# Prompt attention over three strided branches of 75 key blocks a head in place of one masked pass of 136

## The reference

```python
DILATIONS = ((128, 1), (512, 4), (2048, 16))
    parts = [dilated_branch_prompt(qb, kb, vb, w // d, d) for w, d in DILATIONS]
...
def merge_dilations(parts):
    ms = jnp.stack([m for _, m, _ in parts])
    mx = jnp.max(ms, axis=0)
    wts = jnp.exp(ms - mx)
    num = sum(wts[i][..., None] * parts[i][0] for i in range(len(parts)))
    den = sum(wts[i] * parts[i][2] for i in range(len(parts)))
    return num / den[..., None]
```

## Time and profile before

| | before |
|---|---|
| median of 3 runs | 2519.24 us |
| span of the profiled execution | 2518.4 us |
| TensorE busy | 2218.1 us, 88% |
| VectorE busy | 933.1 us, 37% |
| ScalarE busy | 770.4 us, 31% |
| GpSimd busy | 315.0 us, 13% |
| stage `mixers` | 1102.5 to 2071 us |

### The profile page before, as it was taken

How to read it: one execution, slowest core, us unless ns; L and a number is a source line. 1 busy time by engine, 2 the same in 40 slices (tenths; PEclk the granted TensorE clock), 3 DMA queues, 4 the chain that set the end, 5 groups by cost and what they waited for, 6 DMA issues and landing times. The chain is left out here.

```text
span 2518.4 us, 40099 instructions
## 1 busy us (share of the span) xinstructions
PE 2218.1 (88%) x13254; PEld 1826.2 (73%) x13254; DVE 933.1 (37%) x2542; ACT 770.4 (31%) x1793; POOL 315.0 (13%) x332
## 2 busy tenths in 40 slices
PE   4787989899989989449998999899989986799997
PEld 3676878687868768139897989798979884466664
DVE  5440133114212411235454545455554544132221
ACT  5321122112112211124444444353534442222221
POOL 5200000000000000111111111111212114111110
PEclk9988999999999999769998999999999995899999
DMA  4526352735456373570404040404040104464641
GB/s 134 160 79 200 108 184 72 218 104 169 142 153 180 79 211 98 65 160 27 101 27 102 26 102 27 102 27 101 26 102 26 35 22 133 138 192 133 192 142 59
DMA packets 197558, 274.10 MB, mean 109 GB/s; under 512 B 37237, under 2 KB 159605, under 8 KB 188677
## 3 DMA queue, kind: packets, MB, share of 16 engines
q1 hardware_dynamic: 188852, 204.74, 30.9%
q0 software_dynamic: 1280, 66.98, 7.8%
q10 hardware_dynamic: 7248, 0.03, 0.2%
HBM read 201.70 MB, written 136.87 MB: 134 GB/s over the span
## 5 line engine op out<-in xcount | busy, mean ns | idle before, releaser
L265 PE MATMUL pj<-hT_hi,w_hi 128*128 128x512 f32 (+1 forms) x1056 | 427.9, 405 | 20.4 <-DVE w_lo L470 20.4
L266 PE MATMUL pj<-hT_lo,w_hi 128*128 128x512 f32 (+1 forms) x1056 | 417.0, 395 | 0.0
L267 PE MATMUL pj<-hT_hi,w_lo 128*128 128x512 f32 (+1 forms) x1056 | 416.0, 394 | 0.0
L1173 ACT ACTIVATE pt<-pt_ps 128x512 f32<-128x512 f32 (+2 forms) x320 | 170.9, 534 | 425.4 <-PE pt_ps L1116 425.2
L1124 PEld LDWEIGHTS o_ps<-vt,pt 128*128 128x128 f32 x2176 | 284.5, 194 | 18.6 <-issue 7.4
L1124 PE MATMUL o_ps<-vt,pt 128*128 128x64 f32 x2176 | 284.0, 271 | 0.0
L1251 DVE CUSTOM_DVE_ANT_0 sc<-s_ps,win 128x512 f32<-128x512 f32 (+2 forms) x320 | 193.0, 610 | 175.0 <-PE s_ps L1100 138.0
L265 PEld LDWEIGHTS pj<-hT_hi,w_hi 128*128 128x128 f32 (+1 forms) x1056 | 198.5, 188 | 67.7 <-DVE w_lo L470 18.2
L267 PEld LDWEIGHTS pj<-hT_hi,w_lo 128*128 128x128 f32 (+1 forms) x1056 | 198.1, 188 | 47.4 <-issue 0.6
L266 PEld LDWEIGHTS pj<-hT_lo,w_hi 128*128 128x128 f32 (+1 forms) x1056 | 198.7, 188 | 42.3 <-issue 0.6
L1167 ACT ACTIVATE sc<-sc,nmax 128x512 f32<-128x512 f32 (+2 forms) x320 | 207.9, 650 | 36.2 <-DVE nmax L1255 36.2
(11 more groups left out here) (358 smaller groups left out, 3190.5 us busy)
## 6 DMA issues: line engine op xcount, KB each, us to landing
out_dram<-in_cache_k_win_dram POOLq DMA_DIRECT2D x8, 4088.0 KB, 15.3
out_dram<-in_cache_v_win_dram POOLq DMA_DIRECT2D x8, 4088.0 KB, 27.7
w_raw<-in_w_in_dram SPq DMA_DIRECT2D x35, 512.0 KB, 9.6
qk_ch<-sil SPq DMA_DIRECT2D x32, 256.0 KB, 6.9
z_ch<-xr SPq DMA_DIRECT2D x32, 256.0 KB, 2.5
wqk<-hi SPq DMA_DIRECT2D x32, 256.0 KB, 3.2
wqk<-lo SPq DMA_DIRECT2D x32, 256.0 KB, 3.5
out_dram<-xr SPq DMA_DIRECT2D x32, 256.0 KB, 2.8
```

The lines of the kernel that those rows point to most:

```text
L265: pe.matmul(out, w_hi[s][:, k, 0:m], hT_hi[:, k, cols], start=(k == 0), stop=False)
L266: pe.matmul(out, w_hi[s][:, k, 0:m], hT_lo[:, k, cols], start=False, stop=False)
L267: mm = pe.matmul(out, w_lo[s][:, k, 0:m], hT_hi[:, k, cols], start=False, stop=(k == KT - 1))
L1173: act.activation(pt[:, n % 4, 0:w], pt_ps[turned_bank((step, qb, *a[1:]))[0]][:, 0:w], ACT.Copy).then_inc(S["turned_out"], 1)
```

## The change

Each branch becomes a banded attention of its own. A query tile is 128 tokens at stride 1, 4 or 16 (`tile_tokens`); it reads its own key tile and, in branches 0 and 1, the one before, so 31 + 28 + 16 = 75 key blocks. Strided tiles are read straight from `qs`, `kh` and `kl` with a step. Tiles are packed into units of up to 512 columns, 20 a head; 4 tiles of numerators share a bank of `o_ps`. The mask is one table `E.band` of 256 columns. The values have a 65th column of ones in three layouts (three loads a head instead of one, in rows of 256 bytes), so the mix gives the row sum too. The scores' negated maximum stands in a 66th column.

Branches 0 and 1 are copied to `stg`, stored to DRAM in rows of 264 bytes and read back so that a partition holds 16 consecutive tokens, as branch 2's tiles do (`round_trip`, on SyncE's queue). Per head, `weigh` makes the three weights, `merge` multiplies (GpSimd two branches, VectorE the third) and adds. `flip` comes once a pair and 512 columns wide. `weigh` and `merge` of the first head lie inside the body, those of the second at its end with the four flips; twelve delta steps are held back for that place. The tables for `sample` move into `gates`.

```diff
-            for e in range(2):
-                load_head_from(sp, D, env, e, e)
-                load_chunk_from(sp, D, env, e, e)
+            load_head_from(sp, D, env, 0, 0)
+            for b in range(3):
+                load_values_from(sp, D, env, 0, b)
+            load_chunk_from(sp, D, env, 0, 0)
+            load_chunk_from(sp, D, env, 1, 1)
+            load_head_from(sp, D, env, 1, 1)
+            load_gate_from(sp, D, env, 0)
...
+            then(pool.memset(E.band[:], 0.0))
+            select(E.band[:, 0:P], ALU.is_ge, NEG, 0, [[1, P]], -1)
+            select(E.band[:, P:2 * P], ALU.is_ge, NEG, 0, [[-1, P]], 1)
...
+PART = HD + 2
+DILATE = (1, 4, 16)
+TILES = NT
+
+
+def tile_tokens(b, t):
+
+    if b == 0:
+        return P * t, 1, t > 0
+    if b == 1:
+        return CHUNK * (t // 4) + t % 4, 4, t >= 4
+    return t, 16, False
+
+
+def units_of(b):
+
+    if b == 0:
+        return [(2 * x, 2 * x + 1) for x in range(8)]
+    if b == 1:
+        return [(r + 4 * x, r + 4 * x + 4) for r in range(4) for x in (0, 2)]
+    return [tuple(range(4 * x, 4 * x + 4)) for x in range(4)]
...
+HEAD_UNITS = [(b, tiles) for b in range(3) for tiles in units_of(b)]
+NU = len(HEAD_UNITS)
+UNITS = [(e, b, tiles) for e in range(2) for b, tiles in HEAD_UNITS]
...
+HEAD_GROUPS = ([(0, 2 * g, 2 * g + 1, tuple(range(4 * g, 4 * g + 4))) for g in range(4)]
+               + [(1, 8 + 2 * r, 8 + 2 * r + 1, tuple(r + 4 * x for x in range(4))) for r in range(4)]
+               + [(2, 16 + x, 16 + x, tuple(range(4 * x, 4 * x + 4))) for x in range(4)])
...
+def pair_order():
+
+    order = [("score", 0), ("score", 1), ("exp", 0)]
+    N = 2 * NU
+    for n in range(N + 1):
+        if n < N:
+            order.append(("turn", n))
+            if n + 1 < N:
+                order.append(("exp", n + 1))
+            if n + 2 < N:
+                order.append(("score", n + 2))
+        if n:
+            order.append(("mix", n - 1))
+            g, _, last = group_of(n - 1)
+            if last:
+                order.append(("out", g))
+        if n == NU + 6:
+            order += [("weigh", 0)]
+        if n == NU + 9:
+            order += [("merge", 0)]
+    tail = [("weigh", 1), ("merge", 1)] + [("flip", x) for x in range(4)]
+    cost = {"score": 5, "turn": 4, "mix": 9, "flip": 4}
+    delta = [("delta", u, s) for u in range(4) for s in DELTA_STEPS]
+    held = delta[-12:]
+    delta = delta[:-12]
+    total = sum(cost.get(s, 0) for s, *_ in order)
+    woven, spent, given = [], 0, 0
     for step in order:
         woven.append(step)
+        spent += cost.get(step[0], 0)
+        upto = len(delta) * spent // total
         woven += delta[given:upto]
         given = upto
+    for k, step in enumerate(tail):
+        woven.append(step)
+        woven += held[2 * k:2 * k + 2]
     return woven
...
+    vt = [sb(f"vt{b}", [P, TILES, HD + 1]) for b in range(3)]
+    zb = sb("zb", [P, SEQ])
...
+def load_values_from(sp, D, env, h, b):
+
+    vt, v_in = env.operands[3][b], env.v_in[b]
+    v = D.new_v[:, bass.ds(HD * h, HD)]
+    if b == 0:
+        sp.dma_start(vt[:, :, 0:HD], v.rearrange("(n p) d -> p n d", p=P)).then_inc(v_in, 16)
+    elif b == 1:
+        for x in range(4):
+            sp.dma_start(vt[:, 4 * x:4 * x + 4, 0:HD], v[CHUNK * x:CHUNK * (x + 1)].rearrange("(p r) d -> p r d", r=4)).then_inc(v_in, 16)
+    else:
+        sp.dma_start(vt[:, :, 0:HD], v.rearrange("(p r) d -> p r d", r=16)).then_inc(v_in, 16)
...
+        NS_C, NP_T = 3, 2
+        sc = sb("sc", [P, NS_C, CHUNK])
+        pt = sb("pt", [P, NP_T, CHUNK])
+        stg = [sb(f"stg{b}", [P, TILES, PART]) for b in range(2)]
+        all3 = sb("all3", [P, 3, TILES, PART])
+        om = sb("om", [P, TILES, 2, HD])
...
+            def round_trip(i, e, b, more):
+
+                h = 2 * i + e
+                sp.wait_ge(S["o_out"], O_CREDIT + NGR * h + 4 * b + 4)
+                sp.sem_inc(S["seen"], 1)
+                if b == 0:
+                    dst = D.part[b, bass.ds(h, 1)].rearrange("a (n p) c -> p (a n) c", p=P)
+                    sp.dma_start(dst, stg[b][:]).then_inc(part_stored[b], 16)
+                else:
+                    for x in range(4):
+                        dst = D.part[b, bass.ds(h, 1), CHUNK * x:CHUNK * (x + 1)].rearrange("a (p r) c -> p (a r) c", r=4)
+                        sp.dma_start(dst, stg[b][:, 4 * x:4 * x + 4, :]).then_inc(part_stored[b], 16)
+                if more:
+                    load_values_from(sp, D, env, h + 1, b)
+                sp.wait_ge(part_stored[b], (16, 64)[b] * (h + 1))
+                sp.wait_ge(S["om_made"], h + 1)
+                sp.sem_inc(S["seen"], 1)
+                sp.dma_start(all3[:, b], D.part[b, bass.ds(h, 1)].rearrange("a (p r) c -> p (a r) c", r=16)).then_inc(part_in[b], 16)
+
+            def pair(i, more):
                 for e in range(2):
-                    store(i, e, True)
-            for e in range(2):
-                store(SW_HEADS // 2 - 1, e, False)
+                    h = 2 * i + e
+                    round_trip(i, e, 0, more or e == 0)
+                    store_chunk(i, e, 0, more)
+                    round_trip(i, e, 1, more or e == 0)
+                    store_chunk(i, e, 1, more)
+                    if more or e == 0:
+                        sp.wait_ge(S["mixed"], S_CREDIT + NU * (h + 1))
+                        sp.sem_inc(S["seen"], 1)
+                        load_values_from(sp, D, env, h + 1, 2)
+                    if more:
+                        load_head(h + 2, e)
+                sp.wait_ge(S["gated_b"], NF + NF * (i + 1))
+                sp.sem_inc(S["seen"], 1)
+                sp.dma_start(D.mix[bass.ds(P * i + QK_W, P), :], zb[:]).then_inc(z_stored, 16)
+                if more:
+                    sp.wait_ge(z_stored, 16 * i + 16)
+                    load_gate_from(sp, D, env, i + 1)
...
+                    elif step == "merge":
+                        h = 2 * i + a[0]
+                        pool.wait_ge(S["weighed"], h + 1)
+                        x = all3[:, 0:2, :, 0:HD]
+                        pool.tensor_tensor(x, x, wts[:, 0:2].unsqueeze(3).to_broadcast([P, 2, TILES, HD]), ALU.mult).then_inc(S["part_scaled"], 1)
...
+                        for t, at, w in unit_blocks(n):
+                            first, d, back = tile_tokens(b, t)
+                            q = qs[e][:, first:first + d * (P - 1) + 1:d]
+                            k0 = first - d * P * back
+                            keys = slice(k0, first + d * (P - 1) + 1, d)
+                            pe.matmul(s_ps[n % 2][:, at:at + w], q, kh[e][:, keys], start=True, stop=False)
+                            mm = pe.matmul(s_ps[n % 2][:, at:at + w], q, kl[e][:, keys], start=False, stop=True)
+                        mm.then_inc(S["scores"], 1)
...
+                        if opens:
+                            pe.wait_ge(S["o_out"], 2 * NGR * i + g + 1)
+                        if n % NU in (0, 8, 16):
+                            pe.wait_ge(v_in[b], 16 * VALUE_DMAS[b] * (2 * i + e + 1))
+                        for t, at, w in unit_blocks(n):
+                            j = members.index(t)
+                            for x in range(w // P):
+                                back = w // P - 1 - x
+                                key_tile = t - back * (1, 4, 1)[b]
+                                mm = pe.matmul(o_ps[g % 2][:, (HD + 1) * j:(HD + 1) * (j + 1)], pt[:, n % NP_T, at + P * x:at + P * x + P], vt[b][:, key_tile, :],
+                                               start=(x == 0), stop=(back == 0))
...
+                    elif step == "flip":
+                        s = bank_free(i, ("flip", n))
+                        pe.wait_ge(S["om_made"], 1 + 2 * i + 2)
+                        pe.sem_inc(S["seen"], 1)
+                        for x in range(4):
+                            mm = pe.transpose(pt_ps[s][:, P * x:P * x + P], om[:, 4 * n + x, :, :].rearrange("p e d -> p (e d)"), ident[:])
+                        mm.then_inc(S["flipped"], 1)
...
+                        act.wait_ge(S["masked"], S_CREDIT + 2 * NU * i + n + 1)
+                        for t, at, w in unit_blocks(n):
+                            x = sc[:, n % NS_C, at:at + w]
+                            ins = act.activation(x, x, ACT.Exp, scale=-1.0, bias=home(b)[:, t, HD + 1:HD + 2])
+                        ins.then_inc(S["exped"], 1)
...
+                    elif step == "out":
+                        h, g = 2 * i + n // NGR, n % NGR
+                        b, _, last, members = HEAD_GROUPS[g]
+                        act.wait_ge(S["mixed"], NP_T + NU * h + last + 1)
+                        if g % 4 == 0:
+                            if b < 2:
+                                act.wait_ge(part_stored[b], (16, 64)[b] * h)
+                            else:
+                                act.wait_ge(S["om_made"], h + 1)
+                        if b == 1:
```

(74 more changed lines are left out.)

301 lines of the change are left out of this document (125 added, 176 removed).

## The result

| | before | after |
|---|---|---|
| median | 2519.0 us | 2548.1 us |
| range, 4 runs each | 2517.6 to 2520.8 | 2543.3 to 2549.4 |
| ratio, 95% interval | | 1.0111 (1.0096 to 1.0125) |
| span of the profiled execution | 2518.4 us | 2547.1 us |
| stage `mixers` | 968.5 us | 1004.9 us |

The forecast was 2439 us, with 2515 as the high end. The stage was to take 889 us and took 1004.9. It begins 8.6 us earlier, at 1093.9, because `gates` became shorter; 1004.9 - 968.5 - 8.6 is 27.8 of the 28.7 us between the spans.

The account below looks back on a forecast made before the run. The TensorE's in-order issue was taken to bound `mixers`. A pair summed to 167.8 + 6.4 + 17 + 7 + 17 + 1 + 6 = 222.2 us against 242.1; four pairs save 79.7, so 2439 us, range 2370 to 2515.

Parts of the forecast that it names:

- issue of the TensorE at full speed, unit reads: TensorE instructions of a pair in `mixers`: 167.8 us with fewer blocks, 51.2 less than before.
- strided reads: Query and key reads of branches 1 and 2: no cost taken; bounds nothing to 15.4 us a pair.
- clock: Work at the 1.2 GHz level around more idle stretches: 6 us a pair (2 to 12).
- small gaps: Gaps beside the TensorE's waits in a pair: 8.4 us before, shrinking with the work to 6.4.
- the delta chain in the body: Delta steps with less attention work between them: 5 us open a chunk, 17 a pair (5 to 41).
- the merge: Head 0's merge in mid-body, VectorE waiting for GpSimd's product: 7 us (4 to 10).
- the tail: End of a pair after the last mix: 29.7 us, TensorE issuing 13.0, idle 17 (12 to 25).
- the refill: The pair fills once, where before each head did: 1 us.
- The delta chain as the pace: Rival: half the chain's waiting open (41.5 us), a pair 246.7, kernel 2538 us; chance 0.12.
- The trip through DRAM: Branch 1 of head 1, store and read back: 11 to 16 us, hidden, with 0 to 5 exposed.
- Gates: Loads before the loop, gate stage moving about the same bytes: 0, plus or minus 3 us.
- rival one: Strided score reads in branches 1 and 2 cost double: 62 us more, 2501 us; chance 0.11.

Follow-up runs that it names:

- the last kernel above: The change with branch 1 and 2 queries laid out by GpSimd and the merge's sums made a later step of their own: 2443.6 us, again 2433.4 us (0.9652).
- unit keys: The change with only the keys of branches 1 and 2 read at a step of one, queries still strided: 2558.3 us (1.0155).
- the small merge: The change with the merge's products on GpSimd and VectorE cut to one tile of sixteen, sums kept: 2523.7 us (1.0016).
- both reads at unit step: The change with queries and keys of branches 1 and 2 read at a step of one: 2517.7 us (0.9974).
- Added work of two kinds: 512-column matmul or narrow 128 by 128 product ahead of branch 1 and 2 units, queries and keys at unit step: 2460.7, 2459.9 us; the former in the change: 2536.3.
- filling the waits: The change with overwritten 128 by 128 products added where the TensorE waits for GpSimd at a delta chunk's change: 2596.3 us (1.0303).

## Why the prediction was wrong

Step by step, per pair of heads:

| term | forecast | measured |
|---|---|---|
| issue of the TensorE at full speed, unit reads | 167.8 | not apart |
| strided reads | 0 | 13.9 |
| clock | 6 | about 37, with the next row |
| small gaps | 6.4 | in the row above |
| TensorE busy in all | 180.2 | 873.2 / 4 = 218.3 |
| waits | 17 + 7 + 17 + 1 = 42 | 131.7 / 4 = 32.9 |
| pair | 222.2 | 251.2 |

*Counts and prices* held: 1200 mix instructions at 0.11, 256-wide matmuls at 0.12 in branch 0. With 167.8 taken as right, 218.3 - 167.8 - 13.9 = 36.6 is left for the clock and for whatever else is in it; the estimate from the windows gives 134 / 4 = 33.4.

*The small gaps* were misread. The prediction takes 8.4 us a pair before as gaps beside the waits. But the waits alone, 14.7, are all of the idle time before (60 us, 15 a pair), so those 8.4 lay in the busy time of the TensorE, and 27 / 4 = 6.8 of them are what the clock cost there. They scaled with the work to 6.4 in the sum. So what the prediction held for the clock is at most 6 + 6.4 = 12.4 us a pair.

*Strided operands* is the first step that failed. I took the low end of my bounds, nothing, because the stream of a 256-wide matmul had slack beside its weight load. The stride was in the weights too, so the thing that set the pace was itself slowed. The high end, a doubling worth 15.4 us a pair, was nearly exact: 13.9. The rule of the Trainium skill ("SBUF — State Buffer", section "Door 1: The DMA port swizzle"), that an access which crosses to a new line of 16 bytes pays, agrees with 0.215 for 0.11. At 56 us this is the smaller part of the miss.

*The clock* is the step that failed most: 6 us a pair were forecast, 12.4 with the misread gaps, and about 37 came, so 24.2 more a pair and 97 in the stage. I had read the row at a loop boundary as "the clock is low where the TensorE idled" and costed the new idle stretches. For the short low stretches around idle time that was about right (half of 267 - 148 = 119 us busy, 15 us a pair). What came on top was another thing, long stretches at the 1.2 GHz level in which it is fully busy: half of 148 us, 18.5 a pair. The Trainium skill ("TensorE: Matmul & The Clock Gate", section "Part 1: The HAM clock gate") has the clock low by default and activity releasing it; by that alone the clock would be expected to stay in stretches of 34 us with rows of 5.00 busy of 5. It does not, and the rows decide.

*Waits* were over-estimated, 33 us for 42. The second pair shows which: the delta chain in the body about 7 for 17, near the low bound of 5; the merge 7.7 for 7; the tail 15.0 for 17; the refill 3.4 for 1. The delta chain as the pace, the slower rival, did not happen: 37 us of chain waits a pair were its point, and all waits together stay below. The merge's parts were mis-sized: GpSimd's product 4.66 for 4.2, the first sum 2.05 for 1.25. In the change GpSimd starts an operation of 1.03 us (L1079) just ahead of that sum; in the last kernel above, where this operation is over before, the same sum takes 1.22. *The trip through DRAM* is hidden, as said. Its rows of 264 bytes are slow, 7.3 us for 528 KB against 3.0 for 512 KB; the rule on short descriptors that the prediction cites from the Trainium skill ("DMA: Bandwidth & Descriptors", section "Specifications") agrees with that row, and nothing waits for it. *Gates* gave 8.6 us where I allowed 3.

So the stage is the forecast plus rival one, plus the miss of the clock, minus idle time: 889 + 56 + 97 - 36 = 1006 us, for 1004.9. With the waits as they were, neither miss alone passes the 2515 us of the high end (2439 + 97 - 36 = 2500 and 2439 + 56 - 36 = 2459); both together do. The version with both repairs runs at 2433, near the 2439 of the forecast, but by compensation: its stage of 884.6 us has 27 us of idle time a pair for 42, and about 14 lost to the clock, where 12.4 were allowed; its keys are still strided.

What stays open is what sets off a long stretch. Within one kernel it begins at the same place of the order in most pairs. In the change, and in its versions with unit keys and with the small merge, that is the end of branch 1 of head 0, in 11 pairs of 12; with both reads at unit step it is branch 0 of head 1 in three pairs of four, behind the change of a delta chunk. The first profile of the split merge has it there in one pair, the second in none. The same sparse 5 us lie before it and before places where it doesn't come. Added work of two kinds removed it in one kernel; in the change one kind didn't, and filling the waits made two of it. That it hangs on how the waits fall in time fits all of this and is argued, not shown.

## What to carry to other kernels

Before a matmul operand gets a stride, ask which of its two reads sets the pace: weights of 128 strided columns took 0.22 us in place of 0.11 here, and of the streams beside them here only one of 512 columns hid it. Let an idle engine lay such an operand out, and split a step in which one engine waits for another's long product, so that queued work goes between. When a change adds waits to a dense stage of the TensorE, carry a term for busy time at the 1.2 GHz level, not only for work near idle gaps: here it cost an estimated 134 us of a stage of 1005, against 27 of 968 before. And when a change of a read moves the time, look at the granted clock before the read gets the credit.

## What the runs showed of the hardware

- Strided weights at a step of 4 or 16 took 0.215 to 0.22 us for 128 columns, against 0.11, and at the 1.2 GHz level also 0.22; a strided stream of 256 columns took 0.23 to 0.24, against 0.12.
- The granted clock fell to 0.50 for 34 to 41 us with the TensorE busy in all but 0.5 of them. The kernel with both reads at unit step, which has such stretches too, took from 2488 to 2523 us from run to run.
- 21 us of added, useless matmuls made one kernel 57 us faster; in another, 28 us of them made it 48 us slower, of which the clock is 27 by the estimate.
